# A 24-column weight tile laid out twice: two matmuls per contraction eighth in place of three

## The reference, cut to what matters

```
x = x + 0.5 * SwiGLU_1(RMSNorm(x))
h = RMSNorm(x); P = h @ w_in        # one projection, columns split into 4 head groups
o = concat[RWKV7(P_rw), RGLRU(P_rg), GatedDeltaNet(P_gdn), GLA(P_gla)]
x = x + o @ w_out
x = x + 0.5 * SwiGLU_2(RMSNorm(x))
```

## Time and profile before

| what | value |
|---|---|
| median of 3 runs | 1352.9 us (1351.08 to 1353.68) |
| the profiled execution, its own time | 1353.87 us |
| its span, first to last instruction | 1352.1 us |
| TensorE matmul busy | 1329.3 us (98%), 12584 instructions |
| TensorE weight load busy | 1289.2 us (95%) |
| VectorE busy | 855.8 us (63%), 1327 instructions |
| ScalarE busy | 692.6 us (51%), 995 instructions |
| GpSimd busy | 77.4 us (6%) |
| DMA | 185.90 MB, mean 137 GB/s |
| mean granted TensorE clock | 0.997 |

### The profile page before, as it was taken

The page is one execution under the profiler, slowest core; times in us unless marked ns, Lnnn a source line. Parts: engine busy times, 40 slices in busy tenths (PEclk is TensorE's granted clock), DMA queues, the critical chain, the costliest instruction groups (busy, mean ns, idle before and its releaser), DMA issues.

```text
span 1352.1 us, 31424 instructions
## 1 busy us (share of the span) xinstructions
PE 1329.3 (98%) x12584; PEld 1289.2 (95%) x12584; DVE 855.8 (63%) x1327; ACT 692.6 (51%) x995; POOL 77.4 (6%) x113
## 2 busy tenths in 40 slices
PE   7999999999999999999999999999999999999997
PEld 7999999998988999999999999999888899999997
DVE  6656533898876756553376565349988766555533
ACT  7444423757655644443364444347466655454423
POOL 0000000200030100000010000001001310000001
PEclk9999999999999999999999999999999999999999
DMA  8544454322313644444454444443223244444541
GB/s 302 173 143 150 144 155 155 111 79 80 112 50 111 212 145 150 146 154 154 142 189 153 155 143 152 151 144 110 80 79 97 66 158 156 155 148 147 155 142 53
DMA packets 50768, 185.90 MB, mean 137 GB/s; under 512 B 5760, under 2 KB 6272, under 8 KB 50176
## 3 DMA queue, kind: packets, MB, share of 16 engines
q1 hardware_dynamic: 49104, 177.37, 41.3%
q10 hardware_dynamic: 1584, 7.35, 1.5%
HBM read 180.14 MB, written 4.56 MB: 137 GB/s over the span
## 4 chain that ended last, share of the span: by engine, by line
PE 86%; DVE 11%; issue 2%; ACT 1%; DMA 0%; DVEq 0%; ACTq 0%
PE ps L479 27%; PE ps L481 26%; PE ps L480 26%; DVE wl L1592 2%; DVE ar L1749 2%; PE ps L847 1%; DVE ar L1663 1%; PE ps L749 1%; PE ps L1035 0%; DVE raw L1967 0%; PE ps L817 0%; PE ps L1013 0%; PE ps L799 0%; DVE ar L1740 0%; DVE ar L1683 0%
## 5 line engine op out<-in xcount | busy, mean ns | idle before, releaser
L479 PE MATMUL ps<-xh,wh 128*128 128x320 f32 x1952 | 611.8, 313 | 9.0 <-DVE xl L1614 8.0
L1592 DVE TENSOR_TENSOR wl<-raw,wh 128x1024 fp32r<-128x1024 f32 x332 | 408.1, 1231 | 317.5 <-ACT wh L1186 317.1
L481 PE MATMUL ps<-xh,wl 128*128 128x320 f32 x1952 | 604.4, 310 | 0.0
L480 PE MATMUL ps<-xl,wh 128*128 128x320 f32 x1952 | 604.3, 310 | 0.0
L1186 ACT ACTIVATE wh<-raw 128x1024 fp32r<-128x1024 f32 x332 | 349.3, 1054 | 356.2 <-PE ps L481 339.1
L479 PEld LDWEIGHTS ps<-xh,wh 128*128 128x128 f32 x1952 | 367.5, 188 | 20.1 <-issue 9.0
L480 PEld LDWEIGHTS ps<-xl,wh 128*128 128x128 f32 x1952 | 367.7, 188 | 0.5
L481 PEld LDWEIGHTS ps<-xh,wl 128*128 128x128 f32 x1952 | 367.6, 188 | 0.0
L479 PE MATMUL ps<-hid_h,wh 128*128 (+1 forms) x704 | 217.5, 309 | 0.0
L480 PE MATMUL ps<-hid_l,wh 128*128 (+1 forms) x704 | 217.5, 309 | 0.0
L481 PE MATMUL ps<-hid_h,wl 128*128 (+1 forms) x704 | 217.5, 309 | 0.0
(11 more groups left out here) (290 smaller groups left out, 934.6 us busy)
## 6 DMA issues: line engine op xcount, KB each, us to landing
raw<-wts SPq DMA_DIRECT2D x332, 512.0 KB, 3.5
ms<-mst ACTq DMA_DIRECT2D x2, 1440.0 KB, 7.9
mout<-ms ACTq DMA_DIRECT2D x2, 1440.0 KB, 6.6
x<-xT SPq DMA_DIRECT2D x4, 320.0 KB, 4.9
yT<-x SPq DMA_DIRECT2D x4, 320.0 KB, 2.4
cs<-cst SPq DMA_DIRECT2D x1, 652.0 KB, 8.1
pr<-par ACTq DMA_DIRECT2D x1, 429.0 KB, 4.2
pr<-par ACTq DMA_DIRECT2D x1, 425.0 KB, 5.3
```

The lines of the kernel that those rows point to most:

```text
L479: pe.matmul(out, a, rh, start=start, stop=False)
L480: pe.matmul(out, a, rl, start=False, stop=False)
L481: return pe.matmul(out, b, rh, start=False, stop=stop)
L1592: tt(wl[:, s, :], raw_of(layer, n), wh[:, s, :].bitcast(F32), ALU.subtract).then_inc(lo_ready.sem, 1)
```

## The change

Tile 3 gets its 24 columns twice: `b` at 0, `a` at 32, `gd` at 36 (in place of 64), and the same again 64 partitions higher. VectorE's low split of this tile works on the upper 64 columns of each eighth alone, and writes them over the upper half of `wh` in place (512 elements per partition in place of 1024). One stationary tile then holds high weights in columns 0 to 63 and low weights in columns 64 to 127. TensorE runs two matmuls for each eighth with it, by `xh` and by `xl`: 16 in place of 24 for the tile. (The upper half so gets low weights by low activations too, which was not computed before.) The result's two halves are added: ScalarE copies partitions 64 to 127 of the bank into `lnt[0:64]` (a new instruction, between its sigmoid of the low-rank input and `split_hi` of tile 6), VectorE adds that to partitions 0 to 63, waits for itself, and multiplies by `rstd`. These two instructions on VectorE (`small_evac`) take the place of `evac(3)`, and stand later: behind the two subtractions of `rw_mix(2, 4)` in place of ahead of them.

The GLA gate now reads partitions 32 to 63 of `small` with a matrix `glg` of 32 rows (16 of them filled), a further 128 columns of the parameter tile `pr`. The buffers move a little to make room, and three signals share one semaphore, in the order in which they were given before.

```diff
@@ norm_tiles (TensorE)
+                if base == IN0:
+                    small_tile(layer)
+                    return
                 for k in range(KT):
                     ins = part(RING - 1, k)
+                ins.then_inc(unit_used.sem, 1)
+
+            def small_tile(layer):
+
+                pe.wait_ge(lo_ready.sem, layer * UNITS + IN0 + T_SMALL + 1)
+                pe.wait_ge(x_new.sem, layer * 24 + T_SMALL + 1)
+                pe.wait_ge(xl_ready.sem, layer * 24 + 2 * KT)
+                for k in range(KT):
+                    both = wsl(slot(layer, IN0 + T_SMALL), k)[0]
+                    pe.matmul(ps[:, T_SMALL, 0:TOK], both, xh[:, k, :], start=k == 0, stop=False)
+                    ins = pe.matmul(ps[:, T_SMALL, 0:TOK], both, xl[:, k, :], start=False, stop=k == KT - 1)
                 ins.then_inc(unit_used.sem, 1)
@@ gla_gate (TensorE)
-                ins = pe.matmul(ps[:, 6, 0:TOK], P("glag", 0, 128)[64:80, :], small[64:80, :], start=True, stop=True)
+                ins = pe.matmul(ps[:, 6, 0:TOK], P("glg", 0, 128)[32:64, :], small[32:64, :], start=True, stop=True)
@@ ScalarE
                 say(act.activation(xm[64:128, 6, :], xm[64:128, 6, :], ACT.Sigmoid), "lora_in")
+                act.wait_ge(unit_used.sem, layer * UNITS + IN0 + T_SMALL + 1)
+                say(act.activation(lnt[0:64, :], ps[64:128, T_SMALL, 0:TOK], ACT.Copy), "small_low")
                 ahead(2)
@@ split_lo (VectorE)
-                tt(wl[:, s, :], raw_of(layer, n), wh[:, s, :].bitcast(F32), ALU.subtract).then_inc(lo_ready.sem, 1)
+                low, of, high = wl[:, s, :], raw_of(layer, n), wh[:, s, :]
+                if n == IN0 + T_SMALL:
+                    of, high = (v.rearrange("q (k m) -> q k m", k=KT)[:, :, 64:128] for v in (of, high))
+                    low = high
+                tt(low, of, high.bitcast(F32), ALU.subtract).then_inc(lo_ready.sem, 1)
@@ VectorE
+                def small_evac():
+
+                    on(ve, layer, "small_low")
+                    rows = slice(0, 64)
+                    st(tt(small[rows, :], ps[rows, T_SMALL, 0:TOK], lnt[rows, :], ALU.add))
+                    st.settle()
+                    st(tt(small[rows, :], small[rows, :], rstd[rows, :], ALU.mult), in_read)
...
-                def rw_mix(lo, hi):
+                def rw_mix(lo, hi, between=None):
...
                     st(tt(seqs(xm[:, lo:hi], 0), seqs(rwp[:, lo:hi], 1, 0), seqs(rwp[:, lo:hi], 1, 1), ALU.subtract))
                     st.settle()
+                    if between:
+                        between()
                     for k in range(lo, hi):
...
                 evac(2)
-                evac(3)
-                rw_mix(2, 4)
+                rw_mix(2, 4, small_evac)
@@ signals and buffers
-    "rw_P": 1, "kk_rn": 1, "rb": 1, "rw_ops": 1, "kPi": 1, "bPi": 1, "bonus": 1,
+    "rw_P": 1, "kk_rn": 1, "rb": 1, "rw_keyed": ("bPi", "rw_ops", "kPi"), "bonus": 1,
-        lkd, ltm, lmin = (A(u, 320) for u in (79, 24, 25))
+        lkd, ltm, lmin = (A(u, 320) for u in (78, 24, 25))
```

More of the change, by code:

```diff
@@ L92 @@
     ("gnw", 1), ("glw", 1), ("alog", 1), ("dtb", 1), ("gb", 1), ("lora", 256), ("glag", 256),
-    ("wa", 128), ("wx", 128)])
+    ("wa", 128), ("wx", 128), ("glg", 128)])
 CST, CSTN = columns([
@@ L110 @@
 MIX_SIGNALS = {
-    "padded": ("pads", "rg_pads"), "xm": 7, "lora_in": 1, "lora_mm": 3, "sg": 2, "ra": 2,
+    "padded": ("pads", "rg_pads"), "xm": 7, "lora_in": 1, "lora_mm": 3, "small_low": 1, "sg": 2, "ra": 2,
     "rw_gc": 2, "shift_kept": 1, "kkraw": 2, "kk_sq": 1, "rkr": 2, "head_sums": ("kk_sum", "rk_sum", "gdn_sum"), "cum": 2, "prev": 1,
-    "rw_P": 1, "kk_rn": 1, "rb": 1, "rw_ops": 1, "kPi": 1, "bPi": 1, "bonus": 1,
+    "rw_P": 1, "kk_rn": 1, "rb": 1, "rw_keyed": ("bPi", "rw_ops", "kPi"), "bonus": 1,
     "rw_pairs": 2, "rw_pairs_read": 6,
@@ L127 @@
 }
-V_STEPS, A_STEPS, G_STEPS = 102, 51, 14 + 3 * 6
+V_STEPS, A_STEPS, G_STEPS = 103, 51, 14 + 3 * 6
 G_ALL = DEPTH * G_STEPS - 6
@@ L208, in program @@
             pass
-        ar = sb("ar", [128, 80 * TOK])
+        ar = sb("ar", [128, 73 * TOK + 6 * CVP])
         ps = ctx.enter_context(nc.psum_tensor("ps", [128, 8, 512], F32))
@@ L1667, in evac @@
                     else:
-                        dst = small if m == T_SMALL else gla[:, m - T_GLA, :] if m < T_RG else gz[:, m - T_Z, :] if m < T_GT else \
+                        dst = gla[:, m - T_GLA, :] if m < T_RG else gz[:, m - T_Z, :] if m < T_GT else \
                             gt[:, m - T_GT, :] if m < T_RGG else rgg[:, m - T_RGG, :]
@@ L2456, in lay_out @@
         b0 = GDN0 + 4 * GW
-        for at, src, n in ((0, b0, NH), (32, b0 + NH, NH), (64, GLA_GD, 16)):
-            tw[:, T_SMALL * 128 + at:T_SMALL * 128 + at + n] = w[:, src:src + n]
+        for at, src, n in ((0, b0, NH), (32, b0 + NH, NH), (36, GLA_GD, 16)):
+            for first in (T_SMALL * 128 + at, T_SMALL * 128 + 64 + at):
+                tw[:, first:first + n] = w[:, src:src + n]
         wts += ffn(1) + [cols(crossed(tw, CROSSED_IN, 1)), cols(crossed(i["w_out"][l], (0, 7), 0))] + ffn(2)
@@ L2479, in lay_out @@
     put("lora", np.concatenate([i["rwkv_w2"], i["rwkv_a2"], i["rwkv_g2"]], 1))
-    par[:, 64:80, PAR["glag"][0]:PAR["glag"][0] + 128] = i["gla_g2"]
+    par[:, 36:52, PAR["glg"][0]:PAR["glg"][0] + 128] = i["gla_g2"]
     for h in range(NH):
```

## The result

Eleven runs of each kernel on the same chip: the changed kernel takes 1356.47 us in the median (1353.40 to 1359.13), the kernel before 1352.24 (1350.81 to 1353.92). The ratio is 1.0027, 95% interval 1.0019 to 1.0035: slower by 2.6 to 4.7 us, best 3.6 (the two medians lie 4.2 us apart). I had forecast 1.04 us, 1353.9 in the median, and no change that can be told; the median lies above the stated range of 1351.0 to 1356.0. The profiled run of the changed kernel took 1356.84 us, its span 1355.0; the kernel before 1353.87 and 1352.1.

What follows compares the result with a forecast made beforehand. VectorE's gapless stream was taken to bound the mixing stage, so only its evacuation counted: +0.52 us in each of 2 layers, +1.04 us, 1353.9 us in the median. Range of 8 in 10: 1351.0 to 1356.0.

Steps and rivals of the forecast that it cites:

- What bounds the kernel: In the mixing stage's start VectorE's own gapless stream decides; TensorE, though busy, has 0.5 us to spare at the last gate.
- TensorE's part: Tile 3 loses 8 matmuls per layer, 1.17 us, lost again in waits: nothing gained; bounds 0 to 1.17 us per layer.
- VectorE's evacuation: Tile 3's add and multiply in place of one evacuation: +0.52 us per layer, bounds +0.40 to +0.7.
- ScalarE's copy: Tile 3's copy ends between 258.3 and 258.45, ahead of VectorE's add at 258.51: no wait, 0.1 us to spare.
- The moved signal: The fourth `in_read` comes at 259.5 in place of 257.9, before TensorE, ScalarE or GLA's gate needs it: no wait.
- the shorter low split: VectorE's low split of tile 3 is about 0.5 us shorter, but the gain falls in an idle gap: nothing.
- the parameters: 128 more parameter columns load 0.6 us longer, landing at about 15.4 us against first need at 20.72: nothing.
- The sum: Over both layers 2 * 0.52 = +1.04 us, to a median of 1353.9 us, +0.08%; forecast's chance 0.72.
- TensorE setting the end: Rival: TensorE sets the stage's end, so the 8 matmuls come off in full, 2.34 us, to 1350.6 us; chance 0.08.
- the extra taken up: Rival: slack in VectorE's stream or the shorter low split absorbs its extra time: 1352.9 us; chance 0.12.
- the late hand-over: Rival: ScalarE's copy lands behind 258.51 and VectorE stands at the add in both layers: 1355.5 us; chance 0.08.
- Two products do not take the time of three: Rival, here denied: tile 3's two products take three's time, TensorE gains nothing, still 1353.9 us; chance within the forecast's.

Runs made afterwards that it cites:

- e3: Kernel before with tile 3's evacuation as two VectorE instructions in the later place, three products, no ScalarE copy: 1353.93 us, ratio 1.0012 to the kernel before.
- e4: Changed kernel without ScalarE's copy, with one evacuation instruction at the old place, so only the 16 matmuls remain: 1354.08 us, ratio 1.0011 to the kernel before.
- e6: Kernel before without the decoding chunk's products of one group in each layer, 16 matmul records fewer in all: 1356.38 us, ratio 1.0021.
- e10: Kernel before with the decoding chunk's products of one group kept but cut from 128 columns to 2, instruction count unchanged: 1353.46 us, ratio 1.0003.
- e1: The changed kernel again without any edit, timed against the kernel before: 1354.80 us, ratio 1.0020.
- e5: Changed kernel plus 8 unread matmuls of 2 columns in tile 3 per layer, restoring the instruction count: 1354.13 us, ratio 1.0005 to the kernel before.
- e11: Changed kernel plus 4 unread matmuls of 2 columns in tile 3 per layer: 1353.75 us, ratio 1.0010 to the kernel before.

## Why the prediction was wrong

**What bounds the kernel**: right within the stage, and by its mechanism. VectorE's 0.55 us per layer was paid in full (74.07 against 73.52, e3 the same), TensorE's relief was not (e4's stage is 73.51).

**TensorE's part**, priced at nothing: right as to the gain. Tile 3's sixteen matmuls run from 252.76 to the next tile's first at 255.34, and the low-rank matmuls start at 258.95. The 1.17 us turned into waits at evacuations and low splits, as the step said. Its bounds, 0 to 1.17 us gained, excluded a loss without giving a reason, and e4 shows a loss: +1.5 us (0.3 to 2.6), with VectorE's chain in the stage as before.

**VectorE's evacuation**, +0.52: measured +0.55. **ScalarE's copy**, hidden with 0.1 us to spare: hidden with 0.17. **The moved signal, the shorter low split and the parameters**, nothing: no wait for any of them shows, and from its first evacuation to the gate VectorE still waits for nobody in either layer. The gap ahead of tile 4's low split grew from 0.66 to 1.19 us, as forecast.

**The sum** is the step that failed. It took the time outside the stage as unchanged: "2 layers * 0.52 = +1.04 us". It lacked a term for where TensorE's instructions stand in the program. Sixteen instructions fewer ahead of and between the dense parts cost 2.4 us in a kernel without the change (e6 against e10), 1.5 us by e4, and putting sixteen near-empty ones back took the changed kernel from 1.0020 to 1.0005 (e1, e5), 2.0 us. With the chain's 1.1 us this makes 2.6 to 3.5 of the 3.6 measured. The kernel before's trace had the rows for it, in neither the chain's leading lines nor the stage that I read: three stops on issue worth 2.0 us behind it, and one stretch at the low clock. I had read none of them, since I looked only at what the change touches. From them the size could not have been worked out, but the term belonged in the range, whose upper end of 1356.0 the median passed by 0.5 us.

**The rivals.** TensorE setting the end, the extra taken up, and the late hand-over all fell: the first by the wait left at the gate, the second by the stage, the third by the add that starts without a releaser. Two products do not take the time of three: tile 3's starts are 0.147 us apart. None of the four was the mechanism that decided.

What stays open: why 16 fewer is the expensive count while 8 fewer, none and 16 more are not. The traces lead one step further back, to a fetch that begins later with this count (ahead of record 10356 when TensorE is at record 10304 to 10351, against 10254 to 10286 in the other ten kernels), but not to why it does. Open too is why the stops of one kernel vary from run to run (e1 and the changed kernel are the same program, with 5.1 and 1.7 us of them), and why e4 and e6, with the same count and the same stage, come out at 1.0011 and 1.0021; their intervals overlap.

## What to carry to other kernels

Where a stage is set by one engine's own stream, the rows around an edit give its price to a few hundredths of a microsecond, and relief on the other engine, here 1.17 us per layer, is worth nothing in time. But taking instructions out is itself an edit: on a stretch in which TensorE runs hundreds of tiny matmuls, stops without a releaser move over the work with the instruction count, and so does their length, and a change of some tenths of a percent can't be judged before the same count has been tried with near-empty instructions. Read the stops on issue, the clock and the packets of kind instruction over the whole run before calling the rest unchanged.

## What the runs showed of the hardware

In the dense parts TensorE stands for 0.2 to 2.0 us without a releaser at fixed numbers of its instruction stream, neighbours 127 or 128 matmul records apart: four instructions taken out ahead move the stop by exactly four matmuls (x10 in e5, x6 in e11 and, for eight, x2 in e1), whatever their work. Each of the 56 stops of 0.15 us or more ends 1.1 to 1.6 us behind the end of a packet of 16,384 bytes on the queue of kind instruction; the packet itself takes 0.9 to 1.6 us.

The granted clock fell from 2.4 to 1.2 GHz for 3.4 us at a time, in places that were nearly, not exactly, the same from kernel to kernel: behind the last gate of a mixing stage (between 996 and 1004 us in nine of the table's fourteen kernels, 330 to 336 in the changed kernel alone), and in the dense part at stops of 0.9 to 2.0 us (384 to 390 us in the changed kernel, 1062 to 1068 in e1 and e4), but not at each of them: e6 has none at its stop of 1.8 us. Each such stretch costs up to 1.7 us.
